# Ln and Exp from one function set on ScalarE, in a two-block network on one core

## The reference, cut to what matters

```
for each of 2 layers:                                  # first block
    h = rms_norm(x); q, k, v, z, xbc, dt = split(h @ w_in)
    attention (8 heads, softmax of 512 keys) on rotated, normed q and k
    Mamba-2 scan in 4 chunks of 128, both directions: silu(conv(xbc)), softplus(dt), exp of decays
    x += concat(attention, rms(y * silu(z))) @ w_out
    x += (silu(h @ w_gate) * (h @ w_up)) @ w_down      # h = rms_norm(x)
x = rms_norm(x)
x += 0.5 * ffn(rmsnorm(x))                             # second block
u = rmsnorm(x); proj = u @ w_in_mix + b
  HGRN2 over 8 heads:  f = sigmoid(hf), log f, cumulated, exp of differences; rmsnorm per head
  LRU over 8 heads:    a = exp(-8 * sigmoid(..) * softplus(..)); scan; times gelu(lg)
  conv branch:         31 taps on ca * sigmoid(cb); layernorm; silu
x += (sum of sigmoid(gate_i) * (branch_i @ w_branch_i)) @ w_out
x += 0.5 * ffn(rmsnorm(x));  out = rmsnorm(x)
```

## Time and profile before

| | us |
|---|---|
| median of 3 runs | 3129.86 (3125.75 to 3130.39) |
| profiled execution, its own time | 3128.58 |
| its span, first to last instruction | 3126.8 |
| PE busy in the span | 2874.6 (92%) |
| DVE busy | 1682.7 (54%) |
| ACT busy | 1307.7 (42%) |
| mean granted clock of PE | 0.963 |

### The profile page before, as it was taken

The page is one execution under the profiler, slowest core; times in us unless marked ns, Lnnn a source line. Parts: engine busy times, 40 slices in busy tenths (PEclk is TensorE's granted clock), DMA queues, the critical chain, the costliest instruction groups (busy, mean ns, idle before and its releaser), DMA issues.

```text
span 3126.8 us, 31460 instructions
## 1 busy us (share of the span) xinstructions
PE 2874.6 (92%) x12578; PEld 2272.5 (73%) x12578; DVE 1682.7 (54%) x2318; ACT 1307.7 (42%) x1817; POOL 20.9 (1%) x41
## 2 busy tenths in 40 slices
PE   7899999999899999999999988877799956999998
PEld 5555888887556888888888877656677744888886
DVE  4668444344578444444443466777566686544433
ACT  6545423225555323234222366655467514332222
POOL 0000000000000000000000000000000000000000
PEclk9899999999899999999999999989899977999999
DMA  4100332233101222232223421111122311222231
GB/s 176 54 21 2 121 98 98 95 95 120 47 21 41 95 99 97 93 103 90 99 93 98 140 74 54 56 39 48 42 95 86 115 47 41 96 100 95 97 95 64
DMA packets 71617, 253.07 MB, mean 81 GB/s; under 512 B 8112, under 2 KB 9136, under 8 KB 71088
## 3 DMA queue, kind: packets, MB, share of 16 engines
q1 hardware_dynamic: 67968, 236.38, 23.0%
q0 software_dynamic: 2352, 12.58, 1.1%
q10 hardware_dynamic: 1152, 2.10, 0.2%
HBM read 242.64 MB, written 8.39 MB: 80 GB/s over the span
## 4 chain that ended last, share of the span: by engine, by line
PE 75%; DVE 13%; ACT 9%; issue 3%; ACTq 0%; DMA 0%; DVEq 0%; SPq 0%
PE PS L1141 21%; PE PS L1143 21%; PE PS L1142 21%; DVE CVA L2101 3%; ACT WHI L1373 2%; PE PS L1281 2%; PE PS L1294 2%; DVE XBC L1806 1%; PE PS L1266 1%; DVE SAC L2069 1%; DVE WLO L1718 1%; PE PS L1159 1%; PE PS L1103 1%; PE PS L1160 1%; PE PS L1161 1%
## 5 line engine op out<-in xcount | busy, mean ns | idle before, releaser
L1141 PE MATMUL PS<-HHI,WHI 128*128 128x512 f32 x2288 | 921.4, 403 | 14.9 <-ACT Z L1436 10.9
L1142 PE MATMUL PS<-HLO,WHI 128*128 128x512 f32 x2288 | 899.4, 393 | 0.0
L1143 PE MATMUL PS<-HHI,WLO 128*128 128x512 f32 x2288 | 899.1, 393 | 0.0
L1718 DVE TENSOR_TENSOR WLO<-WR,WHI 128x1024 fp32r<-128x1024 f32 (+1 forms) x446 | 537.6, 1206 | 622.8 <-ACT WHI L1373 618.9
L1373 ACT CAST WHI<-WR 128x1024 fp32r<-128x1024 f32 (+1 forms) x446 | 457.7, 1027 | 255.2 <-PE PS L1143 244.4
L1141 PEld LDWEIGHTS PS<-HHI,WHI 128*128 128x128 f32 x2288 | 436.0, 191 | 126.4 <-issue 24.9
L1142 PEld LDWEIGHTS PS<-HLO,WHI 128*128 128x128 f32 x2288 | 436.1, 191 | 92.8 <-issue 5.7
L1143 PEld LDWEIGHTS PS<-HHI,WLO 128*128 128x128 f32 x2288 | 434.8, 190 | 92.4
L1141 PE MATMUL PS<-FHI,WHI 128*128 128x512 f32 x704 | 273.9, 389 | 0.0
L1142 PE MATMUL PS<-FLO,WHI 128*128 128x512 f32 x704 | 273.9, 389 | 0.0
L1143 PE MATMUL PS<-FHI,WLO 128*128 128x512 f32 x704 | 273.9, 389 | 0.0
(11 more groups left out here) (350 smaller groups left out, 3092.1 us busy)
## 6 DMA issues: line engine op xcount, KB each, us to landing
WR<-in_stream SPq DMA_DIRECT2D x414, 512.0 KB, 3.3
WR<-in_stream SPq DMA_DIRECT2D x32, 384.0 KB, 3.0
xkeep<-X POOLq DMA_DIRECT2D x3, 2048.0 KB, 9.6
X<-xkeep POOLq DMA_DIRECT2D x24, 256.0 KB, 6.2
X<-in_xin ACTq DMA_DIRECT2D x8, 256.0 KB, 7.7
out<-X SPq DMA_DIRECT2D x8, 256.0 KB, 2.1
GW<-in_gates SPq DMA_DIRECT2D x8, 128.0 KB, 3.2
RT<-in_rope SPq DMA_DIRECT2D x2, 320.0 KB, 4.5
```

The lines of the kernel that those rows point to most:

```text
L1141: e.matmul(out, hi[:, i, :], xhi, start=first, stop=False)
L1142: e.matmul(out, hi[:, i, :], xlo, start=False, stop=False)
L1143: t = e.matmul(out, lo[:, i, :], xhi, start=False, stop=final)
L1718: e.tensor_tensor(lo, raw, hi.bitcast(F32), ALU.subtract).then_inc(S["dve_low"], 1)
```

## The change

ACT's program keeps account of the function set that it needs. Where a step of the kinds listed under `LOG_EXP` follows one of another set, it writes an explicit load of the set `natural_log_exp_and_others`, at the head of the step, ahead of that step's waits. For Silu, Sigmoid and Gelu it writes none; their loads are left to the build. The ledger keeps the same account: at each change of set it moves ACT's end on by 1.28 us, and the times of the steps that hold such functions are lowered, since their loads are no longer part of them. No other engine's instructions change but by the order of the steps.

```diff
-... "root": (("act", 4.0),),
+... "root": (("act", 1.4),),
-    "rroot": (("act", 3.9),), ... "gsq": (("act", 3.9),),
+    "rroot": (("act", 1.35),), ... "gsq": (("act", 1.2),),
-    ... "rln": (("act", 2.6),), "eb": (("act", 1.9),),
+    ... "rln": (("act", 1.25),), "eb": (("act", 1.8),),
-    ... "roroot": (("act", 3.9),), ... "gelu": (("act", 2.0),),
+    ... "roroot": (("act", 1.35),), ... "gelu": (("act", 0.69),),
-    "gact": (("act", 4.7),), ... "croot": (("act", 3.9),),
+    "gact": (("act", 2.0),), ... "croot": (("act", 1.35),),
-    "dta": (("dve", 0.3), ("act", 3.0), ("dve", 0.2), ("act", 1.4), ("dve", 1.0)),
+    "dta": (("dve", 0.3), ("act", 0.5), ("dve", 0.2), ("act", 0.3), ("dve", 1.0)),
-    ... "lru1": (("act", 4.0), ("dve", 0.1)), "lru2": (("dve", 0.7), ("act", 2.0)),
+    ... "lru1": (("act", 2.0), ("dve", 0.1)), "lru2": (("dve", 0.7), ("act", 0.65)),
+LOG_EXP = "natural_log_exp_and_others"
+FUNCTIONS = {
+    **dict.fromkeys("root rroot dta ex dexp gsq exp small rln dd eb roroot lru1 lru2 croot".split(), LOG_EXP),
+    **dict.fromkeys("silu zsilu xsilu cvsilu qsilu gsilu".split(), "silu"),
+    **dict.fromkeys("fk qsig gsig cbsig gact bsig".split(), "sigmoid"),
+    "gelu": "gelu",
+}
 # class Order, in __init__ and in add, ahead of the loop over TIMES
+        self.functions = None
+        if FUNCTIONS.get(step[0], self.functions) != self.functions:
+            self.functions = FUNCTIONS[step[0]]
+            self.engine_end["act"] += 1.28
 # scalar_engine
+        functions = None
         for step in o.steps:
             kind, *a = step
+            if FUNCTIONS.get(kind, functions) != functions:
+                functions = FUNCTIONS[kind]
+                if functions == LOG_EXP:
+                    e.preload_act_table_set(LOG_EXP)
```

More of the change, by code:

```diff
@@ L145 @@
     "gates": (("pe", 1.72),), "mean": (("pe", 6.9),), "cmm": (("pe", 0.86),),
-    "high": (("act", 1.04),), "uhi": (("act", 0.71),), "hhi": (("act", 0.62),), "sq": (("act", 0.61),), "root": (("act", 4.0),),
+    "high": (("act", 1.04),), "uhi": (("act", 0.71),), "hhi": (("act", 0.62),), "sq": (("act", 0.61),), "root": (("act", 1.4),),
     "silu": (("act", 0.6),), "fhi": (("act", 0.62),), "zsilu": (("act", 0.65),), "conv0": (("act", 0.69),),
     "xsilu": (("act", 0.69),), "raw": (("act", 0.61),), "v": (("act", 0.61),), "rsq": (("act", 0.6),),
-    "rroot": (("act", 3.9),), "xta": (("act", 0.61),), "bt": (("act", 0.61),), "ex": (("act", 0.7),),
-    "dexp": (("act", 0.65),), "gsq": (("act", 3.9),), "exp": (("act", 0.75),), "pta": (("act", 0.68),),
+    "rroot": (("act", 1.35),), "xta": (("act", 0.61),), "bt": (("act", 0.61),), "ex": (("act", 0.7),),
+    "dexp": (("act", 0.65),), "gsq": (("act", 1.2),), "exp": (("act", 0.75),), "pta": (("act", 0.68),),
     "fk": (("act", 1.4),), "qsig": (("act", 0.69),), "ca": (("act", 0.69),), "gsig": (("act", 0.69),),
[L152 to L156, removed]
+    "cbsig": (("act", 0.69),), "rln": (("act", 1.25),), "eb": (("act", 1.8),), "sof": (("act", 1.0),),
+    "rosq": (("act", 0.6),), "roroot": (("act", 1.35),), "yhi": (("act", 0.62),), "cv0": (("act", 0.81),),
+    "cvout": (("act", 0.62),), "lx": (("act", 0.69),), "gelu": (("act", 0.69),), "xb0": (("act", 0.82),),
+    "gact": (("act", 2.0),), "bsig": (("act", 0.69),), "yhs": (("act", 0.62),), "mu": (("act", 0.61),),
+    "csq": (("act", 0.62),), "croot": (("act", 1.35),), "cvsilu": (("act", 0.81),),
     "low": (("dve", 1.23),), "ulo": (("dve", 0.75),), "scale": (("dve", 0.75),), "hlo": (("dve", 0.7),), "acc": (("dve", 0.7),),
@@ L159 @@
     "conv": (("dve", 3.2),), "dt": (("dve", 0.2),), "rnorm": (("dve", 0.75),), "rope": (("dve", 2.2),), "xtd": (("dve", 0.7),),
-    "dta": (("dve", 0.3), ("act", 3.0), ("dve", 0.2), ("act", 1.4), ("dve", 1.0)), "dte": (("dve", 0.4),),
+    "dta": (("dve", 0.3), ("act", 0.5), ("dve", 0.2), ("act", 0.3), ("dve", 1.0)), "dte": (("dve", 0.4),),
     "xd": (("dve", 0.7),), "stadd": (("dve", 1.0),), "ra": (("dve", 1.2),), "mask": (("dve", 0.7),), "xc": (("dve", 1.4),),
@@ L166 @@
     "lqk": (("dve", 0.72),), "pick": (("dve", 0.74),), "xq": (("dve", 1.8),), "xk": (("dve", 0.2),), "ry": (("dve", 1.6),),
-    "ylo": (("dve", 0.7),), "tap": (("dve", 0.75),), "xbt": (("dve", 2.5),), "lru1": (("act", 4.0), ("dve", 0.1)),
-    "lru2": (("dve", 0.7), ("act", 2.0)), "lru3": (("dve", 2.1),), "yl": (("dve", 0.7),), "merge": (("dve", 1.1),),
+    "ylo": (("dve", 0.7),), "tap": (("dve", 0.75),), "xbt": (("dve", 2.5),), "lru1": (("act", 2.0), ("dve", 0.1)),
+    "lru2": (("dve", 0.7), ("act", 0.65)), "lru3": (("dve", 2.1),), "yl": (("dve", 0.7),), "merge": (("dve", 1.1),),
     "yls": (("dve", 0.7),), "cen": (("dve", 0.7),), "cscale": (("dve", 0.7),),
```

## The result

After: 3075.4 us (median of 4 runs, 3074.55 to 3076.68); before, on the same chip, 3130.12. The ratio is 0.9829, 95% interval 0.9814 to 0.9843: 54.7 us faster. I had forecast 3104, 26 us less, and a range that ended at 3083. The direction was right; the gain was twice what I had worked out, and outside the range.

A forecast was written before the change was run, and what follows sets the result against it. PE was taken as the bound, busy 2874.6 of 3126.8 us. Gains of 6.4 (layers), 3.4 (heads), 13.7 (lru) and 2.6 (ends) sum to 26.1 us: 3128.58 to 3102.5, predicted as 3104 for the median; range 3083 to 3128.

The forecast's parts named there:

- What moves: All engines' order under the ledger's new times: costed at nothing, tap counts unchanged, 20 taps either way (15 us) in the range.
- Rival B: Heads and first parts: PE's clock rises as well, giving back 16 of 64 us, time 3087; chance 0.12.
- sum on the path: Gain from removed loads on the chain that ended last: first parts 6.4, heads 3.4, lru 13.7, ends 2.6, together 26.1 us.
- lru term: Lru stage: all 11.1 us of PE's wait for XB goes, plus 2.6 after the last head; 13.7 us.
- layers' term: First parts of the two layers: five loads on the chain go, 6.4 us; bounds nothing and 50.0.
- heads' term: Heads: five loads and 0.34 us on the chain, 6.8 us, half taken, 3.4; bounds nothing and 16.7.
- What goes: ACT's function loads: 81 of 210 go, 129 stay, 103.9 us off ACT's busy time, to about 1204.
- What one is worth: Each load removed between a norm's Ln and Exp on ACT gives 1.3 us, with no drain beside it.
- rival F: Each of the 18 loads on the chain frees twice 1.3 us: gain 47 us, time 3083; chance 0.02.
- E: Rival: the named set isn't honoured on ACT; 3130, or 3147 if named loads come on top; chance 0.05.
- C: Rival: the loads removed in layers and heads were cover; about 8 us gained, 3122; chance 0.15.
- D: Rival: 43 taps move from the heads to behind branch 1, costing 31.4 us; 3139, slower; chance 0.08.

The follow-up runs named there:

- sets only: The kernel before with its old ledger and order of steps, only the function set named on ACT; 3105.9 us, ratio 0.9918 to 0.9948.
- A slack in one comparison: `fill` may place a tap while the ledger's DVE end is up to 0.7 us ahead of its clock; 3013.9, 3045.7 and 3104.7 us on three kernels.
- the account in the first block: The kernel after, with the ledger counting loads only in the first block (the two layers); 3075.5 us, and 3013.9 with 0.7 us of tap slack.
- the five kernels with the same steps in the layers: Kernels with named sets and one step list up to the second block, differing later in account or tap slack; layers 1022.7 to 1027.6 us.

## Why the prediction was wrong

*The step that failed* is "What moves": I took the new order at nothing, with 15 us either way, worked out from the taps alone. It is worth 31 us on top of the sets (spans 3103.8 to 3072.9): 23.8 in the layers, 12.5 in lru, 1.2 in the heads, less 6.9 in the tail. The ledger's account of the loads took 22.9 us out of PE's idle time in the layers (59.2 without it, 36.3 after), and its shorter times made lru shorter. That the layers had such room was to be seen: PE's waits for XBC and PR, 10.9 and 10.2 us, were in the view of the earlier trace rows, and I used three other rows of it. Rival B, the clock, came true in the layers: PE's busy time there fell by 13.5 us with the same matmuls (969.0 to 955.5), 8.4 of it already with sets only. In the heads, where B had half of its low clock's cost, the clock is 0.92 after 0.91. (B's 3087 is 3088 by its own figures.)

*What is worth what.* The sum on the path was right as a sum and not in its parts, and that its two largest errors cancel is luck. Sets only, the step's own test, gave 22.9 us for 26.1: in its profile layers 13.6 (6.4 forecast), heads 2.6 (3.4), lru 6.0 (13.7), tail and end 0.8 (2.6). The lru term was too large since I let two loads less take away the whole wait for XB; with the old order 8.5 of the 11.1 us stayed, and `lru1` still stood behind `bsig` there. That this is the cause is likely and not shown. The layers' term was near for PE's idle time, which fell by 5.2 us (60.2 to 55.0); the other 8.4 us are PE's own busy time, mostly in the second layer's first part, where the clock was 0.97 instead of 0.95, and the sum has no term for that. The heads' term was also read short: the chain that ended last holds two more loads that go, of L1577 at 2088.60 and 2136.53, so 9.3 us there and not 6.8. Half of that is still more than the 2.6 that came.

*What goes.* 81 loads in the old order: sets only has 129 and ACT busy 1204.7 us, as forecast. I gave that number for the kernel after, whose own order has 18 loads more.

*What one is worth* held: 1.28 us of load and the Exp right behind it; 81 loads less took 103.0 us off ACT's busy time, 1.27 each. That speaks against rival F, which had 47 us for the sets where 22.9 came. The drain that the Trainium skill's page "ScalarE: Activation LUTs" has beside the load, in the section "What ACT_TABLE_LOAD costs", does not show in any of these runs: in the kernel before ACT goes on within 0.05 us behind 137 of the 210 loads, and all but three of them begin within 0.02 us of the end of the instruction before. E is out, the named set holds over Ln and Exp in every kernel that names it. C is out: the layers' loads were not cover. D's mechanism is there at a quarter of its size: 11 taps moved behind lru, not 43, and the tail is 6.7 us longer.

## What to carry to other kernels

When the order of a kernel is planned from estimated times, a change of the estimates is a change of its own: try it apart from what it stands for, and price it by the idle time of the bound engine that the plan's order leaves, not by the work that is removed. Count a load where it falls, on the engine's queue, rather than within each step that may need it; here the order that came of it made more of a difference (31 us) than the loads (23). And look at what the plan leaves for the end: work with no cover there cost 0.79 us and more for each 0.73 us instruction. A slack in one comparison gave it back, but how much depended on the order it was put on: 62 us with the account in the first block, 30 on the kernel after, 25 on the kernel before.

## What I had not expected of the hardware

A wait taken away on PE gave back more than its own length. From 31 us to the end of the layers, before and after:

```profile
31.00:1060.20 1029.20, 968.97 (x4159) 719.90 (x4159) 577.76 (x879) 452.66 (x699) 9.15 (x17) 0.97 0.21 68
```

```profile
31.00:1022.80 991.80, 955.51 (x4162) 709.51 (x4161) 577.22 (x879) 399.10 (x655) 9.16 (x17) 0.99 0.21 71
```

PE's idle time fell by 23.9 us, from 60.2 to 36.3, and the stretch got 37.4 us shorter. The other 13.5 us are PE's busy time for the same matmuls, as the granted clock rose from 0.97 to 0.99, a smaller share at 1.2 GHz in place of 2.4. This second part is the less sure one: in the five kernels with the same steps in the layers it varied by 5 us, where the idle time agreed within 0.1. In the whole span PE was busy 13.4 us less and the mean granted clock went from 0.963 to 0.970.
